# First attention of a long fp32 kernel: values become the stationary operand, and GpSimd scales the probabilities

## The reference

```python
def masked_softmax(s, mask):
    ...
    e = jnp.where(mask, jnp.exp(s - m), 0.0)
    return e / jnp.maximum(jnp.sum(e, axis=-1, keepdims=True), 1e-30)

def fox_mixer(q, k, v, f_logit):           # 8 heads, causal, with a forget term in the logits
    ...
        p = masked_softmax(logits, causal[None, None]).astype(v.dtype)
        return jnp.einsum('bhqs,bshd->bqhd', p, v)

def dsa_mixer(q, ckv, k_rope, q_idx, k_idx, w_idx, w_uk, w_uv):   # 8 heads, keys picked by an index score
    ...

def ab_layer(u, w_in, ...):
    ...
    o = jnp.concatenate([o_a.reshape(b, s, -1), o_b.reshape(b, s, -1)], axis=-1)
    return o @ w_out
```

## Time and profile before

| | |
|---|---|
| median of 3 runs | 907.17 us (907.05 to 907.47) |
| span of the profiled execution, first to last instruction | 906.0 us |
| TensorE busy | 888.7 us, 98% |
| VectorE busy | 645.3 us, 71% |
| ScalarE busy | 509.7 us, 56% |
| GpSimd busy | 124.6 us, 14% |
| granted TensorE clock, mean | 1.000 |

### The profile page before, as it was taken

One profiled execution on the slowest core, in us unless ns is written; L12 is line 12 of the kernel. 1 busy time (PEld: TensorE's weight loads), 2 busy tenths in 40 slices (PEclk: granted clock), 3 DMA queues, 4 the chain that ended last, 5 costly groups with the idle time before them and its releaser, 6 DMA issues. The chain is left out here.

```text
span 906.0 us, 14857 instructions
## 1 busy us (share of the span) xinstructions
PE 888.7 (98%) x4796; PEld 743.3 (82%) x4796; DVE 645.3 (71%) x1305; ACT 509.7 (56%) x1017; POOL 124.6 (14%) x168
## 2 busy tenths in 40 slices
PE   8999999999999999999999999999999999999998
PEld 7878787888888888888878888888887778878876
DVE  4768756766666679787467666666876878777785
ACT  6653836445444456686354444444656666666573
POOL 1310300000000000355010000000530401400401
PEclk9999999999999999999999999999999999999999
DMA  9643143656555557101437665555464445454431
GB/s 336 226 150 114 31 157 116 209 191 197 193 188 197 193 186 232 48 25 48 140 116 223 195 189 192 198 185 191 142 221 144 140 140 184 149 179 141 163 116 47
DMA packets 41609, 145.75 MB, mean 161 GB/s; under 512 B 4688, under 2 KB 6224, under 8 KB 41552
## 3 DMA queue, kind: packets, MB, share of 16 engines
q1 hardware_dynamic: 41264, 144.93, 48.2%
q10 hardware_dynamic: 288, 0.07, 0.0%
HBM read 143.93 MB, written 1.05 MB: 160 GB/s over the span
## 5 line engine op out<-in xcount | busy, mean ns | idle before, releaser
L463 DVE TENSOR_TENSOR wl<-raw,wh 128x1024 fp32r<-128x1024 f32 (+2 forms) x270 | 329.3, 1223 | 89.7 <-ACT wh L458 87.0
L458 ACT ACTIVATE wh<-raw 128x1024 fp32r<-128x1024 f32 (+2 forms) x270 | 281.7, 1046 | 66.0 <-PE acc L355 43.3
L353 PE MATMUL acc<-wh,xhl 128*128 128x512 f32 (+1 forms) x472 | 190.8, 404 | 1.3 <-DVE wl L463 0.9
L355 PE MATMUL acc<-wh,xhl 128*128 128x512 f32 (+1 forms) x472 | 184.6, 391 | 0.0
L354 PE MATMUL acc<-wl,xhl 128*128 128x512 f32 (+1 forms) x472 | 184.0, 390 | 0.0
L353 PEld LDWEIGHTS acc<-wh,xhl 128*128 128x128 f32 x472 | 88.7, 188 | 25.8 <-issue 8.0
L355 PEld LDWEIGHTS acc<-wh,xhl 128*128 128x128 f32 x472 | 88.6, 188 | 19.1
L354 PEld LDWEIGHTS acc<-wl,xhl 128*128 128x128 f32 x472 | 88.9, 188 | 16.3
L353 PE MATMUL acc<-wh,hh 128*128 128x512 f32 x256 | 100.2, 392 | 0.0
L354 PE MATMUL acc<-wl,hh 128*128 128x512 f32 x256 | 100.0, 391 | 0.0
L355 PE MATMUL acc<-wh,hl 128*128 128x512 f32 x256 | 99.7, 390 | 0.0
(11 more groups left out here) (302 smaller groups left out, 1350.5 us busy)
## 6 DMA issues: line engine op xcount, KB each, us to landing
raw<-stream SPq DMA_DIRECT2D x266, 512.0 KB, 3.4
raw<-stream SPq DMA_DIRECT2D x4, 352.0 KB, 6.5
h<-x SPq DMA_DIRECT2D x4, 256.0 KB, 4.0
out<-h SPq DMA_DIRECT2D x3, 256.0 KB, 2.1
row<-rows SPq DMA_DIRECT2D x1, 700.0 KB, 9.4
probs<-sel SPq DMA_DIRECT2D x1, 512.0 KB, 8.3
cst<-consts SPq DMA_DIRECT2D x1, 507.0 KB, 7.6
out<-h SPq DMA_DIRECT2D x2, 128.0 KB, 2.0
```

The lines of the kernel that those rows point to most:

```text
L353: nc.tensor.matmul(out_, ah, bh, start=start, stop=False, skip_group_check=True)
L355: return nc.tensor.matmul(out_, al, bh, start=False, stop=stop_, skip_group_check=True)
L458: nc.scalar.activation(used(u, wh[:, u % SPLIT, :]), used(u, raw[:, u % RAW, :]), ACT.Copy).then_inc(w_hi, 1)
L463: nc.vector.tensor_tensor(used(u, wl[:, u % SPLIT, :]), used(u, raw[:, u % RAW, :]), used(u, wh[:, u % SPLIT, :]).bitcast(F32), ALU.subtra ...
```

## The change

1. The values become the stationary operand (`ab_mix`): for each head the 64 columns of its values are loaded, and the transposed probabilities stream past, 256 queries for the first 128 keys, 128 queries for the second. Head 0 writes partitions 0 to 63 of `misc`, head 1 partitions 64 to 127. The result has channels on partitions, tokens in columns: the form in which the output projection takes it.
2. So the result is split straight from `misc`: ScalarE copies the high part to `xh` (`o_high`), VectorE subtracts for the low part (`o_low`). `o_tok`, its transposes and their splits are gone for this attention.
3. As queries are now in columns, 1/sum can't be applied behind the product. VectorE takes the reciprocal (`inverted`), and GpSimd multiplies the probabilities before they are transposed (`weighed`), in place, one instruction for each tile of tokens. `turn_p` waits for that.
4. The units of the first half of the output projection move into and between the last iterations: units 0 and 1 behind iterations 8 and 9, then half of unit 2, the last mix, the other half, unit 3 (`ab_output`). This half now goes to `acc[2]`, `acc[3]`, the other to `acc[0]`, `acc[1]`.
5. Numbers of turned blocks shift by one block (four counts) in all that follows.

```diff
@@ TensorE
             def turn_p(st, a):
-                pe.wait_ge(s_exped, 2 * st + a + 1)
+                if st < STEPS_AB:
+                    pe.wait_ge(s_weighed, T * (st + 1))
+                else:
+                    pe.wait_ge(s_exped, 2 * st + a + 1)
                 pe.wait_ge(s_copied, 2 * st + a)
...
+            def ab_mix(st):
+
+                pe.wait_ge(s_copied, 2 * st + 2)
+                if st >= 1:
+                    pe.wait_ge(s_scaled, st)
+                for c in range(2):
+                    n = (2 - c) * P
+                    for a in range(2):
+                        last = mm(misc[a * HD:(a + 1) * HD, c * P:SEQ], ab_value(st, a, c),
+                                  c_pt(st, a)[:, c * SEQ:c * SEQ + n], start=c == 0, stop=c == 1,
+                                  skip_group_check=True)
+                last.then_inc(s_mixed, 1)
+
+            def ab_output(uu, kks=range(2)):
+
+                u = U_ABO + uu
+                for kk in kks:
+                    k = 2 * uu + kk
+                    if kk == 0:
+                        pe.wait_ge(w_lo, u + 1)
+                    pe.wait_ge(o_hi, k + 1)
+                    for part, (x, w_) in enumerate(((xh, wh), (xh, wl), (xl, wh))):
+                        if part == 2:
+                            pe.wait_ge(s_scaled, k + 1)
+                        for t in range(T):
+                            last = mm(acc[2 + t][:, :], x[:, k, t * P:(t + 1) * P],
+                                      w_[:, u % SPLIT, kk * GW:(kk + 1) * GW], start=k == 0 and part == 0,
+                                      stop=k == KD - 1 and part == 2, skip_group_check=True)
+                    if kk == 1:
+                        last.then_inc(w_used, 1)
...
             for it in range(2, STEPS_AB + DEEP):
                 ab_iter(it)
                 if it in (STEPS_AB, STEPS_AB + 1):
-                    pe_turn_block(pe, 1, o_tok, (it - STEPS_AB,))
...
+                    ab_output(it - STEPS_AB)
+            ab_output(2, (0,))
+            ab_mix(STEPS_AB - 1)
+            ab_output(2, (1,))
+            ab_output(3)
+            second_half(G_ABO, U_ABO, 1, 0)
@@ ScalarE
+            def o_high(st):
+
+                act.wait_ge(s_mixed, st + 1)
+                s_.activation(xh[:, st, :], misc[:, 0:SEQ], ACT.Copy).then_inc(o_hi, 1)
...
                 if 0 <= it - DEEP < STEPS_AB:
                     p_first(it - DEEP)
+                if it - DEEP - 2 >= 0:
+                    o_high(it - DEEP - 2)
                 if it - 1 < STEPS_AB:
                     exponentials(it - 1)
@@ GpSimd
+            def weighed(st):
+
+                pool.wait_ge(s_coef, st + 1)
+                for t in range(T):
+                    n = (t + 1) * P
+                    pb = probs[:, st % DEEP, t * 2 * P:t * 2 * P + 2 * n].rearrange("p (a k) -> p a k", a=2)
+                    g.tensor_tensor(pb, pb, c_stat(rs, st)[:, :, t:t + 1].broadcast_to([P, 2, n]),
+                                    ALU.mult).then_inc(s_weighed, 1)
+
             for it in range(STEPS_AB):
-                coefficients(it).then_inc(s_coef, 1)
+                weighed(it)
@@ VectorE
+            def inverted(st):
+
+                dve.wait_ge(s_exped, 2 * st + 2)
+                v_.reciprocal(c_stat(rs, st), c_stat(su, st)).then_inc(s_coef, 1)
+
+            def o_low(st):
+
+                dve.wait_ge(o_hi, st + 1)
+                v_.tensor_tensor(xl[:, st, :], misc[:, 0:SEQ], xh[:, st, :].bitcast(F32),
+                                 ALU.subtract).then_inc(s_scaled, 1)
 
             for it in range(STEPS_AB + DEEP):
+                if 0 <= it - 2 < STEPS_AB:
+                    inverted(it - 2)
+                if it >= STEPS_AB:
+                    o_low(it - DEEP - 2)
                 if 0 <= it - DEEP < STEPS_AB:
                     p_second(it - DEEP)
-                if it < STEPS_AB - 1:
+                if it < STEPS_AB:
                     ab_peaks(it)
-                if it > DEEP:
-                    ab_scaled(it - DEEP - 1)
...
+                if DEEP + 2 <= it < STEPS_AB:
+                    o_low(it - DEEP - 2)
```

More of the change, by code:

```diff
@@ L291, in program @@
         s_coef, s_scaled, c_added = sem("s_coef"), sem("s_scaled"), sem("c_added")
+        s_weighed, o_hi = sem("s_weighed"), sem("o_hi")
         cmp_scored, parts_added = sem("cmp_scored"), sem("parts_added")
@@ L788, in keep_clock, with second_half @@
                     mm(bank[:, :], zero[:, 0:P], zero[:, :], start=True, stop=True, skip_group_check=True)
-            def output_and_turn(g, u0, b, h0, behind):
-                pe_group(pe, g, u0, 4, GW, block_b=b, after=behind)
+            def second_half(g, u0, b, h0):
                 def turn(uu):
@@ L796, in turn @@
                         pe.wait_ge(h_done, h0 + 2)
-                        pe_turn_block(pe, b + 1, h, (uu - 1,))
-                pe_group(pe, g + 1, u0 + 4, 4, GW, after=turn)
+                        pe_turn_block(pe, b, h, (uu - 1,))
+                pe_group(pe, g, u0 + 4, 4, GW, after=turn)
             def turn_h(b, h0, cc):
@@ L1017, in ab_iter @@
                 if it >= STEPS_AB:
-                    mix(it - DEEP - 1, ab_values(it - DEEP - 1))
+                    ab_mix(it - DEEP - 1)
                 if 0 <= it - DEEP < STEPS_AB:
@@ L1096, in _ @@
                 if it in (STEPS_AB, STEPS_AB + 1):
-                    pe_turn_block(pe, 1, o_tok, (it - STEPS_AB,))
[L1099 to L1109, removed]
+                    ab_output(it - STEPS_AB)
[4 more added lines that the diff above has]
+            second_half(G_ABO, U_ABO, 1, 0)
+            mlp(0, U_M0, 1, 0, 2, H_AB)
             def turn_compress(uu):
@@ L1120, in turn_compress @@
                     last.then_inc(pe_prep, 1)
-            pe_group(pe, G_C, U_C, 4, CQ, block_b=3, after=lambda uu: turn_rest(3, H_AB, uu), late=True)
+            pe_group(pe, G_C, U_C, 4, CQ, block_b=2, after=lambda uu: turn_rest(2, H_AB, uu), late=True)
             pe_group(pe, G_C + 1, U_CQ, 4, GW, after=turn_compress)
@@ L1279, in c_output @@
                     turn_outputs(3)
-            output_and_turn(G_CO, U_CO, 4, H_M0, c_output)
-            mlp(FT, U_M1, 5, H_M0, 6, H_C)
+            pe_group(pe, G_CO, U_CO, 4, GW, block_b=3, after=c_output)
+            second_half(G_CO + 1, U_CO, 4, H_M0)
+            mlp(FT, U_M1, 4, H_M0, 5, H_C)
             E0 = left(G_L)
@@ L1381, in behind @@
                 if s == 0:
-                    turn_rest(6, H_C, u)
+                    turn_rest(5, H_C, u)
                 if s > 0:
@@ L1403, in free @@
                             pe.wait_ge(h_done, H_F + 4 * (s - 2) + 2 * j + 2)
-                    pe_group(pe, j, l_unit(s) + 4 * j, 4, GW, free=free, block_b=6 if s == 0 and j == 0 else None,
+                    pe_group(pe, j, l_unit(s) + 4 * j, 4, GW, free=free, block_b=5 if s == 0 and j == 0 else None,
                              after=lambda uu, j=j: behind(s, 4 * j + uu))
@@ L1633, in _, with ab_last @@
             act.sem_inc(z_act, 2)
-            output_and_turn(U_ABO, 2, G_MLP0)
-            mlp(0, U_M0, N_M0, 3, G_ATTN1)
+            o_high(STEPS_AB - 2)
+            def ab_last(uu):
+                if uu == 0:
+                    o_high(STEPS_AB - 1)
+            output_and_turn(U_ABO, 1, G_MLP0, ab_last)
+            mlp(0, U_M0, N_M0, 2, G_ATTN1)
             act.wait_ge(h_done, H_M0)
@@ L2040, in scaled, with output_and_turn @@
                                  ALU.mult).then_inc(s_scaled, 1)
[L2042 to L2045, removed]
+            def output_and_turn(g0, g1, u0, b, gain, behind):
+                for uu in range(4):
                     split(u0 + uu + LEAD)
-                    dve_turn_block(dve, b - 1, ccs=(uu + 1,))
-                split(u0 + 3 + LEAD)
-                residual_group(g, u0, 4, 0, ahead=False)
+                    behind(uu)
+                residual_group(g0, u0, 4, 0, ahead=False)
                 for uu in range(4, 8):
@@ L2053, in output_and_turn @@
                         dve_turn_block(dve, b, gain, (uu - 5,), KD)
-                residual_group(g + 1, u0 + 4, 4, 1, ahead=False)
+                residual_group(g1, u0 + 4, 4, 1, ahead=False)
                 dve_turn_block(dve, b, gain, (2, 3), KD)
@@ L2258, in _, with ab_last @@
             dve.sem_inc(z_dve, 2)
-            output_and_turn(G_ABO, U_ABO, 2, G_MLP0, lambda: ab_scaled(STEPS_AB - 1))
+            o_low(STEPS_AB - 2)
+            def ab_last(uu):
+                if uu == 0:
+                    o_low(STEPS_AB - 1)
+            output_and_turn(G_ABO + 1, G_ABO, U_ABO, 1, G_MLP0, ab_last)
             for k, (a, b) in enumerate(((R_Q1, R_K1), (R_Q2, R_K2))):
@@ L2424, in _, with c_last @@
             dve.sem_inc(z_dve, 3)
-            output_and_turn(G_CO, U_CO, 5, G_MLP1, lambda: c_scaled(STEPS_C - 1))
-            mlp(FT, U_M1, 6, G_L0)
+            def c_last(uu):
+                if uu == 0:
```

(5 more changed lines are left out.)

46 lines of the change are left out of this document (20 added, 26 removed).

## The result

The change makes the kernel slower: 924.75 us (921.02 to 926.34, 4 runs) against 907.11 for the kernel before on the same chip, a ratio of 1.0182 (95% interval 1.0168 to 1.0196). Forecast were 915.4 and a range of 913.0 to 920.0. The direction was right, the time lies outside the range. The four runs show mean granted clocks of 0.991, 0.985, 0.985 and 0.983; the profiled one is the first, with 921.02 us and a span of 919.2.

What follows compares the result with a forecast made beforehand. The prediction took TensorE's own instructions as the bound. Waits of 16.0 plus own work of 28.9 gave 44.9 us from 93.53, +8.3 on 907.17, so 915.4 us; range 913 to 920.

Steps and rivals of the forecast that it cites:

- first wait, scaled probabilities: TensorE ahead of `turn_p(0,0)`, waiting for GpSimd's weighing, whose reciprocal stands behind VectorE's mask work: 2.67 us.
- `turn_p(1,0)`: TensorE's wait ahead of step 1's first transposes, behind the late `turn_p(0,1)` and `p_second(0)`: 0.91 us.
- `turn_p(2,0)`: TensorE's wait ahead of step 2's first transposes, for `weighed(2)` on GpSimd: 0.48 us.
- mix held by `o_low` behind the peaks: Iterations 5 to 7: `ab_mix` waits for VectorE's `o_low`, queued behind copy and peaks; 2.34 us three times.
- mix held over ScalarE: Iterations 8 to 10: `ab_mix` waits through ScalarE's `p_first` and `o_high`, then `o_low`; 1.65 us three times.
- TensorE's own work: Transposes, scores, value products and output units from 93.53 on: 28.9 us, with 4.9 us removed by the change.
- GpSimd's pair: GpSimd's two products weighing one step's probabilities, 256 and 512 elements per partition: 1.74 us.
- value products of two heads: `ab_mix` on column halves, 8 records, heads overlapping as in the scores: 0.85 us, bounds 0.64 and 1.4.
- The fall of the clock: Rival: TensorE at 1.2 GHz from the first wait in the loop to the first output unit, +9, 924 us; chance 0.07.
- Column halves that don't overlap: Rival: the mix costs 1.28 to 1.4 us, +11.3 to +12.2, total 918.5 to 919.4; chance 0.15.
- GpSimd slower: Rival: GpSimd's pair takes 2.65 us, delaying the first three steps' transposes, +10.1, total 917.3; chance 0.08.
- Mix not held: Rival: the `s_scaled` wait is met early, the six waits (12.0 us) vanish, -3.7, total 903.5; chance 0.05.

Runs made afterwards that it cites:

- The run with the clock held: Changed kernel with products of a zero tile put into TensorE's waits, 9 ahead of the first transposes, 8 or 5 ahead of six mixes; 915.7 us, ratio 1.0090.
- the version with two banks: Changed kernel with value products alternating between `misc` and an idle accumulator bank, each waiting for the split of two steps earlier; 909.9 us, ratio 1.0014.
- low part first: Changed kernel with `o_low` moved ahead of the copy and the peaks on VectorE in iterations 5 to 7; 913.54 us, ratio 1.0064.
- the kernel before, held: Kernel before, with only its first transposes waiting for GpSimd, which first clears a tile seven times; 914.85 us, ratio 1.0061.
- only the first wait filled: Changed kernel with nine zero products ahead of `turn_p(0,0)` alone, the waits ahead of the mix left empty; 921.35 us, ratio 1.0147.
- the order with 1.66: Changed kernel with two banks and early first reciprocal, plus mask work one iteration later and splits of units 0 to 2 moved; 905.9 us, ratio 0.9986.

## Why the prediction was right in its direction and wrong in its size

**The terms at full clock.** The run with the clock held gives the stage without the clock's part. From the first instruction behind the scores (92.95) to the second half (137.25) are 44.3 us, forecast were 44.9, before had 36.6. The waits are those of the kernel after and, where the clock was low there, of this run. The profile counts a wait from the end of the last record; the forecast's sum counted it from where the next instruction could have started, so the table has both.

| term | forecast | measured, as the profile counts | measured, as the sum counts |
|---|---|---|---|
| first wait, scaled probabilities | 2.67 | 2.42 | 2.49 |
| `turn_p(1,0)` | 0.91 | 0.74 | 0.90 |
| `turn_p(2,0)` | 0.48 | 0.14 (101.47 less 100.46 and 0.87) | 0.21 |
| mix held by `o_low` behind the peaks | 3 x 2.34 | 2.18, 2.18, 2.19 | 3 x 2.34 |
| mix held over ScalarE | 3 x 1.65 | 3 x 1.41 | 1.56, 1.50, 1.51 |
| waits together | 16.0 | 14.1 | 15.2 |
| TensorE's own work | 28.9 | | 44.3 - 15.2 = 29.1 |
| GpSimd's pair | 1.74 | 1.61 | |
| value products of two heads | 0.85 | 0.87 for the records | 0.80 |

The waits are sized well, each with its place and its releaser, and so is TensorE's own work, 29.1 for 28.9. The waits were 0.8 too much in the sum, over half of it in the first and in that of `turn_p(2,0)`, as GpSimd's pair was quicker than forecast and its third began earlier. Net +7.7 for +8.3. One comparison in the forecast mixes the two ways of counting: its 0.91 for `turn_p(1,0)` stands beside before's 0.74, which is 0.90 counted as the sum counts, so this wait did not change at all.

**The step that failed** is one that stands in the sum without a number: every duration was taken at 2.4 GHz, though the waits that the same sum forecasts are longer than any idle time seen at full clock in the rows. The fall of the clock stood among the rivals, with a price of 9 and a total of 924, and got a chance of 0.07; the measured median is 924.75. So the step was a cost put at nothing, and it measured 9.8 us in the median (17.6 less the 7.8 with the clock held). That this rival's total comes so near the median is in part luck: its 9 us were to run from the first wait in the loop to the first output unit, and in the profiled execution the first fall began 6 us after that wait had ended and cost 4.4. Its chance was too low. The rows gave no reason for so low a chance: the longest idle time looked at was 1.72, and the forecast had 2.67 once and 2.34 three times, all outside what the rows cover. The range, which ended at 920, left out this case, which the rows did not exclude.

**Where the 13.2 us of the profiled execution are** (span 919.2 against 906.0): the stage takes 141.89 - 93.18 = 48.7 us (93.18 is where the wait of 2.42 begins) instead of 36.6, +12.1. Of these 7.7 are the order of work and 4.4 the first fall of the clock. The stage began 0.35 earlier than before, and some 1.5 remain (13.2 - 12.1 + 0.35) for the second fall at 395. That is a difference; it fits some 3.4 us at half clock there, which do half the work of 3.4 us and so cost 1.7. The kernel before itself lost 1.1 to 1.6 us in the five of its 34 runs whose clock was 0.998. Of the median's +17.6 the order of work has 7.8, measured, and the clock the other 9.8. In the three slower runs, which were not profiled, the clock must have been low for longer, as their means of 0.983 to 0.985 say; where it fell in them was not seen. What exactly brings it down is open too: the length of one idle time, the sum of several and where they lie were not told apart, and the fall at 395 came with none above 0.55 in the 10 us ahead of it.

**The rivals.** Column halves that don't overlap: excluded in either order of the heads. What before took 1.28 takes 0.80 now (from 105.54 to the next transposes at 106.34), near the scores' 0.85. The Trainium skill (TensorE: Matmul & The Clock Gate, Part 3: Packing small matmuls — row/col tiling) says that products on different column groups run at once; the trace agrees, with 0.80 for two heads. GpSimd slower: excluded by 1.61 a pair. Mix not held: excluded by the six waits, and bought back only with a second bank. Of the counter-forecast of 903.5 without these waits, the version with two banks and the clock at 1.000 gives 906.86: some of the waits come back, on ScalarE's copy (0.54 and 0.69) and on GpSimd (0.86), which that case did not count.

**What I said would show me wrong.** The granted clock under 1 came. A mix right behind `turn_p` did not, where a wait was forecast. Eight records over 1.2 us came only at half clock (1.55, at 116.41), which is the same sign once more and none of the column halves.

## What to carry to other kernels

When a change puts a wait on TensorE that is longer than any idle time which the trace shows at full clock, the clock belongs into the sum or at least into the range. An experiment that fills the wait with products of zeros tells its part from the wait's own. A single bank between a producer and a reader turns the reader's order of instructions into TensorE's waits: look for what stands ahead of the reading instruction, before the producer is made faster. Here the new form of the products was worth having (904.96 against 907.9) only after a second bank and one reciprocal moved ahead of work that nobody waited for.

## What was unexpected of the hardware

- One idle time of TensorE of 2.3 to 2.4 us can bring the granted clock to 0.50, and what follows varies between executions of one program: the kernel before with one idle time of 2.27 took 909.71 or 915.74. Added up over stretches of 1 us, the clock of the first attention was at 0.50 for 3.4 us (low part first), 10.2 (two banks), 13.7 (the kernel before, held, and the kernel after) and 20.5 (only the first wait filled).
- With the longest wait of the stage at 1.29, six of seven runs kept 1.000; in the order with 1.66, two of eleven. That the wait decides is not shown.
- Products on column halves overlap whether the heads alternate or one follows the other: 0.82 and 0.81 us from the start of eight records to the next transposes.
